# A decoder step on one Trainium2 core: reworked head, front, norms and router end, with eight products into an unread bank

## The reference

```
u = rmsnorm(h, norm_mix);  proj = u @ w_in          # rq rk rv rg | dqkv | dz | da db | gate_a gate_b
q, k = rotary(rq), rotary(rk);  o_r, s_ret = retention(q, k, rv)      # 4 heads, chunked
branch_a = (rms_plain(o_r) * silu(rg)) @ w_ret_up
conv = silu(causal_conv4(dqkv));  q, k = l2norm(..); g = -exp(a_log) softplus(da + dt_bias); beta = sigmoid(db)
o_d, s_dn = gated_delta(q, k, v, g, beta)           # triangular solve per chunk
branch_b = (rms_plain(o_d) * dn_norm * silu(dz)) @ w_dn_up
h += (sigmoid(gate_a) * branch_a + sigmoid(gate_b) * branch_b) @ w_out
u = rmsnorm(h, norm_ffn);  group = argmax(u @ w_router_group);  top 2 of the group's 4 experts
h += sum over chosen experts of weight * SwiGLU(u)  # 16 experts, 1024 -> 2x256 -> 1024
h += sigmoid(rmsnorm(h) @ w_ple_gate) * (p @ w_ple_proj);  y = rmsnorm(h, norm_final)
```

## Time and profile before

| | us |
|---|---|
| median of 3 runs | 942.37 (939.53 to 943.95) |
| profiled execution | 947.63, span 945.9 |
| TensorE busy | 902.4 |
| VectorE, ScalarE, GpSimd busy | 323.1, 226.9, 133.2 |
| mean granted TensorE clock | 0.977 of 2.4 GHz |
| DMA | 132.96 MB, 141 GB/s mean |

### The profile page before, as it was taken

How to read it: one execution, slowest core, us unless ns; L and a number is a source line. 1 busy time by engine, 2 the same in 40 slices (tenths; PEclk the granted TensorE clock), 3 DMA queues, 4 the chain that set the end, 5 groups by cost and what they waited for, 6 DMA issues and landing times.

```text
span 945.9 us, 11641 instructions
## 1 busy us (share of the span) xinstructions
PE 902.4 (95%) x4753; PEld 590.4 (62%) x4753; DVE 323.1 (34%) x709; ACT 226.9 (24%) x444; POOL 133.2 (14%) x161
## 2 busy tenths in 40 slices
PE   6999979999999999999999998997899999999996
PEld 3456747887889976777777774445444444444452
DVE  3213338876646322440100031334321111102553
ACT  3011325455222311330000001111021111114554
POOL 0423121040154315100000000001100000002100
PEclk9999979999999999999999999997899999999999
DMA  9204603202020202242022234001889999964211
GB/s 379 118 0 161 203 1 134 89 1 97 1 91 3 90 2 96 94 158 77 33 89 89 83 139 170 29 29 66 356 316 378 361 373 369 345 248 167 89 56 45
DMA packets 17764, 132.96 MB, mean 141 GB/s; under 512 B 2272, under 2 KB 2784, under 8 KB 10288
## 3 DMA queue, kind: packets, MB, share of 16 engines
q1 hardware_dynamic: 11600, 103.28, 28.5%
q0 software_dynamic: 5392, 26.38, 7.9%
q10 hardware_dynamic: 720, 2.56, 0.8%
HBM read 115.40 MB, written 21.01 MB: 144 GB/s over the span
## 4 chain that ended last, share of the span: by engine, by line
PE 91%; DVE 5%; ACT 2%; issue 1%; DMA 1%; POOL 0%; SPq 0%; ACTq 0%; DVEq 0%
PE pair L606 35%; PE single L1041 12%; PE pair L1132 7%; PE pair L658 7%; PE pair L952 7%; PE pair L1030 6%; PE pair L1074 2%; PE single L1020 1%; PE single L846 1%; PE single L824 1%; PE single L843 1%; PE single L801 1%; PE pair L752 1%; DMA mem<-in_xT 1%; DVE mem L1565 1%
## 5 line engine op out<-in xcount | busy, mean ns | idle before, releaser
L606 PE MATMUL pair<-mem 128*128 128x288 f32 x1408 | 351.4, 411 | 0.5 <-DVE mem L1675 0.5
L606 PEld LDWEIGHTS pair<-mem 128*128 128x128 f32 x1408 | 269.1, 192 | 80.1 <-issue 2.9
L1041 PE MATMUL single<-mem 128*128 128x512 f32 x256 | 115.3, 604 | 2.2 <-DVE mem L1843 2.2
L1041 PEld LDWEIGHTS single<-mem 128*128 128x128 f32 x256 | 48.3, 194 | 58.0 <-issue 55.2
L1153 ACT ACTIVATE mem<-single 128x256 f32<-128x256 f32 (+4 forms) x96 | 39.1, 416 | 133.4 <-PE single L961 57.4
L1153 ACT ACTIVATE mem<-pair 128x512 f32<-128x512 f32 (+5 forms) x79 | 35.1, 501 | 142.3 <-PE pair L606 64.7
L1132 PE MATMUL pair<-mem 128*128 128x512 f32 (+1 forms) x192 | 65.0, 534 | 1.4 <-DVE mem L1886 1.4
L952 PE MATMUL pair<-mem 128*128 128x512 f32 (+1 forms) x192 | 64.6, 527 | 1.7 <-DVE mem L1689 1.7
L658 PE MATMUL pair<-mem 128*128 128x512 f32 (+1 forms) x192 | 63.9, 524 | 0.4
L1030 PE MATMUL pair<-mem 128*128 128x512 f32 x128 | 57.7, 593 | 1.2 <-ACT mem L1153 1.2
L1836 DVE SCALAR_TENSOR_TENSOR mem<-single,mem 128x256 f32<-128x256 f32 x16 | 7.7, 484 | 146.9 <-PE single L1041 126.3
(11 more groups left out here) (341 smaller groups left out, 941.6 us busy)
## 6 DMA issues: line engine op xcount, KB each, us to landing
mem<-in_w_gu SPq DMA_DIRECT2D x16, 2048.0 KB, 9.2
mem<-in_w_down SPq DMA_DIRECT2D x16, 1024.0 KB, 11.6
y_slots<-mem SPq DMA_DIRECT2D x16, 512.0 KB, 3.1
y_slots<-in_zeros POOLq DMA_DIRECT2D x8, 512.0 KB, 8.3
mem<-in_w_ga SPq DMA_DIRECT2D x2, 2048.0 KB, 8.3
mem<-in_w_gb SPq DMA_DIRECT2D x2, 2048.0 KB, 9.0
mem<-in_w_wo SPq DMA_DIRECT2D x2, 2048.0 KB, 8.2
mem<-in_w_pg SPq DMA_DIRECT2D x2, 2048.0 KB, 11.7
```

Source lines behind the costliest of these rows:

```text
L606: last = nc.tensor.matmul(pb[:, hf, 0:HALF], w(k), rhs[:, k, hf * HALF:(hf + 1) * HALF], start=(k == 0), stop=(k == kk - 1))
L1041: last = nc.tensor.matmul(single[3][:, :], xT[u % 2][:, k, :], w_gu[u][:, k, :], start=(k == 0), stop=(k == KD - 1))
```

## The change

Head: x and the q|k weights come in pieces (HEADK), and the q|k products run block by block over all tiles (`tk`, blocks 0 to 5, then the sums of squares, block 6, `xr`, and block 7 tile by tile as `tmq`), in banks of their own; `qk` has five buffers. The front's steps are reordered. The expanded values are a step of their own (`vx`). gC takes all four prompt tiles in one product. The exponentials are a step for each tile, in blocks 9 and 10, and VectorE's part is `gX`. At level 32 VectorE subtracts in place and ScalarE copies. The addition in `oN` moves from TensorE to VectorE. `x2b` is evacuated by ScalarE, with the square behind it. At the router end eight products of ones by h2, 128x512, are written to a bank that nothing reads (`warm`); two tiles of `idv` go ahead of `x2b`, the others behind gate/up of expert 0; expert 1's transposes go into the middle of that gate/up.

```diff
 def schedule():
-    s = [("ss",)]
+    s = [("tk", k) for k in range(6)] + [("ss",), ("tk", 6), ("xr",)] + [("tmq", t) for t in range(NT)]
     for t in range(NT):
-        s += [("tmq", t)]
-        s += [("rTq", t - 1), ("rTk", t - 1)] if t else [("xr",)]
+        s += [("tmv", t)]
         if t >= 2: s += [("rO", t - 2), ("rU", t - 2)]
-        s += [("tmv", t)]
+        if t < 4: s += [("rTq", t), ("rTk", t)]
         if t: s += [("rS", t - 1)]
-    s += [("rTq", 4), ("rTk", 4), ("rO", 3), ("rU", 3), ("rS", 4)]
+    s += [("rTq", 4), ("rTk", 4), ("rO", 3), ("rU", 3), ("rS", 4), ("vx", 0), ("vx", 1)]
...
-               8: [("gG", t) for t in range(2, NT)] + [("gD", t) for t in range(2, NT)] + [("gE",)],
-               9: [("gs", t) for t in range(3)], 10: [("gs", 3), ("gs", 4)], 11: [("gr",)]}
+               8: [("gG", t) for t in range(2, NT)] + [("gD", t) for t in range(2, NT)],
+               9: [("gs", t) for t in range(3)] + [("gE", 0), ("gE", 1)],
+               10: [("gs", 3), ("gs", 4)] + [("gE", t) for t in range(2, NT)] + [("gX",)], 11: [("gr",)]}
...
-    s += [("x2b", z), ("rank", y), ("rt", z), ("ids", y), ("rtT", z)] + [("idv", t) for t in ORDER[:2]]
-    s += [("rank", z), ("ids", z), ("ovp", 1)] + [("idv", t) for t in ORDER[2:]] + [("cnt",)]
+    s += [("idv", t) for t in ORDER[:2]] + [("x2b", z), ("rank", y), ("rt", z), ("rtT", z), ("ids", y)]
+    s += [("warm", 0)] + [("rank", z)] + [("warm", 1)] + [("ids", z), ("cnt",)] + [("warm", i) for i in range(2, 8)] + [("ovp", 1)]
...
-            sp.dma_start(const[:, 0:HEAD], a["const"][:, 0:HEAD]).then_inc(sem("ld_head"), 16)
-            for k in range(0, KD, 2):
-                sp.dma_start(uT[:, k:k + 2, :], a["xT"][:, k:k + 2, :]).then_inc(sem(f"ld_x{k // 2}"), 16)
-            for k in range(0, KD, 4):
-                sp.dma_start(ring[0][:, 512 * k:512 * k + 2048], a["w_qk"][:, 512 * k:512 * k + 2048]).then_inc(sem(f"ld_qk{k // 4}"), 16)
+            for i, (lo, hi) in enumerate(HEADK):
+                sp.dma_start(uT[:, lo:hi, :], a["xT"][:, lo:hi, :]).then_inc(sem(f"ld_x{i}"), 16)
+                sp.dma_start(ring[0][:, 512 * lo:512 * hi], a["w_qk"][:, 512 * lo:512 * hi]).then_inc(sem(f"ld_qk{i}"), 16)
+                if i == 2:
+                    sp.dma_start(const[:, 0:HEAD], a["const"][:, 0:HEAD]).then_inc(sem("ld_head"), 16)
...
+                elif k0 in ("tk", "tmq"):
+                    k, tiles_ = (s[1], range(NT)) if k0 == "tk" else (KD - 1, [s[1]])
+                    pe.wait_ge(sem("xg"), k + 1)
+                    pe.wait_ge(sem(f"ld_qk{[k < hi for _, hi in HEADK].index(True)}"), 16)
+                    for t in tiles_:
+                        for rows, cols in sides(t):
+                            last = nc.tensor.matmul(q_bank[t][rows, cols], uT[:, k, t * P:t * P + ntok(t)],
+                                                    ring[0][:, 512 * k + cols.start:512 * k + cols.stop],
+                                                    start=(k == 0), stop=(k == KD - 1))
...
-                        if k0 == "oN":
-                            last = nc.tensor.matmul(pb[:, hf, 0:HALF], C("epsq").broadcast_to([P, P]), cs[:, s[1], h],
-                                                    start=False, stop=True)
+                elif k0 == "nq" and s[1] == "oN":
+                    dve.wait_ge(sem("nsq"), q + 1)
+                    dve.wait_ge(sem("q2"), m + 1)
+                    V.scalar_tensor_tensor(out=sq[q % 2], in0=cs[:, m, :], scalar=EPS * DK * DV, in1=sq[q % 2],
+                                           op0=ALU.mult, op1=ALU.add).then_inc(sem("osq"), 1)
...
-                    for t in range(NT):
-                        n = ntok(t)
-                        out = single[plan.buf[s]][0:n, 8 * t:8 * t + 8]
-                        nc.tensor.matmul(out[:, 0:4], tri(t), gl[0:n, t, :], start=True, stop=True)
-                        last = nc.tensor.matmul(out[:, 4:8], C("ones") if t < 4 else C("blk_s", 64), gl[0:n, t, :],
-                                                start=True, stop=True)
+                    for at, w_ in ((0, C("tri")), (16, C("ones"))):
+                        nc.tensor.matmul(out[:, at:at + 16], w_, gl[:, 0:4, :], start=True, stop=True)
+                    for at, w_ in ((32, C("tri_s", 64)), (36, C("blk_s", 64))):
+                        last = nc.tensor.matmul(out[0:64, at:at + 4], w_, gl[0:64, 4, :], start=True, stop=True)
...
+                elif k0 == "warm":
+                    nc.tensor.matmul(single[plan.buf[s]][:, :], C("ones"), h2[:, 0, 0:512], start=True, stop=True).then_inc(s_mm, 1)
...
+            def late_overflow_ids():
+                for t in ORDER[2:]:
+                    last = overflow_ids(t)
+                last.then_inc(sem("idv_mm"), 1)
...
                 for k in range(KD):
                     last = nc.tensor.matmul(single[3][:, :], xT[u % 2][:, k, :], w_gu[u][:, k, :], ...)
+                    if first and u == 0 and k == 3:
+                        xpose(xg_next[0], e + 1, u + 1)
                 last.then_inc(sem("gu_mm"), 1)
-                if nxt:
+                if nxt and not (first and u == 0):
                     xpose(xg_next[0], e + 1, u + 1)
-                if not (first and u == 0):
+                if first and u == 0:
+                    late_overflow_ids()
+                else:
                     down(e - 1, (u - 1) % 4, first and u <= 2)
...
+                elif k0 == "x2b":                     # ScalarE; was a VectorE copy
+                    copy(u2T[POS[t] % 2][:, 4:8, 0:n], ...).then_inc(ev(k0), 1)
                     nc.scalar.activation(sqj[0:n, :], h2[0:n, t, :], ACT.Square, accum_out=ms[0:n, 0, t:t + 1]).then_inc(sem("ms"), 1)
...
+                elif k0 == "lT" and s[1] == 32:       # ScalarE
+                    for r in blocks(t):
+                        last = copy(XT[t][r, :, r], XD[t][r])
+                    last.then_inc(sem("diag"), 1)
...
+                elif k0 == "vx":                      # GpSimd; was in rUs
+                    ev_wait(pool, ("tmv", 4))
+                    for c in range(2):
+                        G.tensor_tensor(vexp[h][0:64, c], ...).then_inc(sem("vexp"), 1)
```

More of the change, by code:

```diff
@@ L220, in __init__ @@
         self.order, self.mm, self.buf, self.before, self.chunk_last, self.norm = {}, {}, {}, {}, {}, {}
-        count, nmm, npair, nsingle, last = {}, 0, 0, 0, {}
+        count, nmm, npair, nsingle, last = {}, 0, 0, 1, {}
         for s in self.steps:
@@ L232, in __init__ @@
                 self.before[s] = None
+            if k in OWN:
+                last.update({key: s for key in own_banks(s)})
             if k in PAIR or k in SINGLE:
@@ L317, in build @@
         cnew = view(MISC + 288, NCONV, 27)
-        qk = [view(slot(0) + 512 * i, 512) for i in range(2)]
+        qk = [view(slot(i), 512) for i in (0, 1, 24, 25, 26)]
         rot = [view(slot(2) + 512 * i, 512) for i in range(2)]
@@ L457, in build @@
         idp = [pair[0][:, 1, 0:2 * NEXP], pair[1][:, 1, 0:8 * NEXP]]
+        q_bank = [pair[t // 2][:, t % 2, :] for t in range(4)] + [single[0]]
+        ss_bank = [single[1][:, 0:HALF], single[2][:, 0:HALF]]
+        xr_bank = single[3]
         def split(ap):
@@ L591, in bank_free @@
                 prev = plan.before[s]
-                if prev is not None:
+                if prev is not None and prev[0] != "warm":
                     ev_wait(pe, prev)
@@ L608, in gemm_channels, with overflow_ids @@
                 last.then_inc(s_mm, 1)
-            pe.wait_ge(sem("ld_head"), 16)
+            def overflow_ids(t):
+                i, n = POS[t], ntok(t)
+                pe.wait_ge(sem("pickm"), 1 if i < 2 else 2)
+                for j in range(2):
+                    at = 128 * (2 * i + j)
+                    last = nc.tensor.matmul(idp[1], pickm[0:n, i, j, :], eov[0:n, at:at + 128],
+                                            start=(i + j == 0), stop=(i + j == NT))
+                return last
             for s in STEPS:
@@ L1027, in down @@
                     pe.wait_ge(sem("y_ready"), 2 * e - 2)
+                elif u == 1:
+                    pe.wait_ge(sem("ids"), 4)
                 for n in range(2):
@@ L1162, in _ @@
                     mm_wait(act, s)
-                    nc.scalar.activation(split(rr[0]), pair576(s), ACT.Sqrt, bias=C("eps"), scale=1.0 / D).then_inc(ev(k0), 1)
+                    for hf in range(2):
+                        last = nc.scalar.activation(rr[0][:, hf * HALF:(hf + 1) * HALF], ss_bank[hf], ACT.Sqrt, bias=C("eps"), scale=1.0 / D)
+                    last.then_inc(ev(k0), 1)
                 elif k0 == "x2a":
@@ L1623, in _ @@
                         last = V.tensor_tensor(X[t][r], X[t][r], src[r], ALU.subtract)
-                    elif v < 32:
+                    else:
                         last = V.tensor_tensor(XD[t], XD[t], src, ALU.subtract)
-                    else:
-                        for r in blocks(t):
```

(1 more changed line is left out.)

155 lines of the change are left out of this document (77 added, 78 removed).

## The result

| | before | after |
|---|---|---|
| median | 943.16 (939.53 to 944.24, 4 runs) | 927.5 (926.08 to 929.0, 4 runs) |
| profiled execution | 947.63, span 945.9 | 926.82, span 925.1 |
| mean granted clock in it | 0.977 | 0.994 |

The ratio is 0.9841, interval 0.9808 to 0.9873: 15.7 us faster, where 27 were forecast. Faster was right; the time lies 4.5 us above the range.

The account below looks back on a forecast made before the run. TensorE's work (902.4 of 945.9 us busy), plus its idling and half clock, was taken as the bound. Eight terms summed to 27.2 us, taking the profiled 947.63 to 920.4; less 5.3 for the median gave 915, range 907 to 923.

Parts of the forecast that it names:

- terms 2: Expanded values moved ahead on GpSimd: TensorE's wait and the half clock behind it go, -10.1 us.
- 3: Cumulated gates (gC) in 4 products: fewer records and less half clock, -2.4 us.
- 4: Exponentials spread over two blocks: the key norms' wait and low clock go, against a new stall, -2.6 us.
- 6: Second norm (oN): each of four norms loses four of eight records, VectorE gets an extra step, -3.2 us.
- 7: Router, tiles 1 to 4: copy of the second half moves from VectorE to ScalarE, -0.5 us.
- term 8: Router end: overflow products moved, earlier gather, faster gate/up; -5 us, from -5.8 at full clock or -3.1 otherwise.
- rival B: Before the kk products: spread exponentials become a new wait, +3 instead of -2.6, 921 us; chance 0.15.
- C: Head starts at full clock and the clock stays full everywhere, 910 us; chance 0.12.
- rival A: Router end: clock falls despite the unread products, which delay the ids; gain 3.1 or less, 917 to 919; chance 0.2.
- Term 5: Inverse level 32: one VectorE subtract instead of two, ScalarE copies the blocks, -0.4 us.
- Sum of part 1: -3.0: Head and front: earlier block-by-block projection 5.1, shorter front waits 0.5, less 2.6 for half clock; bounds -6 and 0.
- The second step: Scaling the whole kernel's time: the profiled execution is 5.3 above the runs' median, so 920.4 becomes 915 us.

Follow-up runs that it names:

- e3: The changed kernel with the head and front of the kernel before; 925.65 us.
- e4: The changed kernel with its new head, but the front's steps in the order of the kernel before; 926.84 us.
- e7: The changed kernel with two more unread 512-column products in waits of the front; 923.61 us, in two groups.
- e6: The changed kernel without its eight products into the unread bank; 929.2 us.
- e13: The kernel before with the new head and front and nothing else of the change; 947.29 us, ratio 1.0049.
- e1: The changed kernel once more, unedited; 925.93 us.
- e9: The changed kernel with the two unread products of e7 in the front and the one of e5 at the router's end; 922.51 us.
- e10: e9 with three products of zeros ahead of the first query and key product; 920.84 us.
- e11: e9 with the middle four of the eight blocks of the query and key product made one; 921.23 us.
- e14: e9 with e11's blocks, products of zeros at the start and one unread product in the tail; 919.46 us, ratio 0.9756.
- e2: The kernel before once more, unedited; 944.82 us.
- e12: e5 with four products of zeros ahead of the row sums; 921.27 us.
- e5: e3 with one more unread product in the router's wait between the last router product and its transpose; 921.22 us.

## Why the prediction was wrong

**What held.** The sign, and terms 2, 3, 4, 6, 7 and 8 to within 1 us each in the profile (table above). Terms 2, 3, 4, 6 and 8 come to 24.3 against 23.3 forecast. The new wait of 1.2 before the kk products is there with 1.4 (L824), and rival B did not come. Nor did C: the first block ran at half clock. The router's end took the full-clock case, 6.0 against 5.8, in the profile; e3, e4 and e7 show that it can as well go the way of rival A, so that this term came in whole is partly luck. Term 5 cannot be read: between 260 and 287 us the profiles of the changed kernel and of e6, which are the same there, differ by 1.8.

**The step that failed: "Sum of part 1: -3.0".** It measured +4.4 in the profile, outside its bounds of -6 and 0, and +4.5 in the medians when alone (e13). No rival put a price on the clock in the front. The miss of 7.4 by its parts, from the rows of both profiles:

- "For the short waits there ... I take 0.5" gained. The waits in the front grew from 0.6 to 2.2, which misses by 2.1. In the new order a block's value product fills a bank, ScalarE empties it only after the state product of two blocks earlier has read the old values (the ScalarE row at 89.12, released by L763), and the scores want that bank. The old order is no cure: in e4, with the wide projections gone from between, the waits were 2.8 at another product.
- The clock in the front, which the sum did not price: 3.0. The records from 91.69 to 96.67 take 4.98 where before they took 3.06, and cv 0 takes 9.15 instead of 8.03. I priced the clock where TensorE starts, and never asked what the wide projections had been doing between the thin products of the front. The profiles of the changed kernel, e1, e6 and e13 have this half clock; in e7, e9, e10, e11 and e14, with wide products in the waits, cv 0 takes 8.03. In e4 it does too, without them, so the waits and thin products make the fall possible and not certain.
- "The projection's records are the same ones reordered": they are, but each follows one into another bank. The projection is 31.4 us of work before and 33.6 after, without the half clock of the first block: 2.2 (e11, for four of the eight blocks: 1.0).
- The first product came at 5.76, not 5.3: 0.5.
- The half clock of the first block, forecast at 2.6, cost 2.2 (5.91 instead of 3.70): 0.4 less.

These come to 2.1 + 3.0 + 2.2 + 0.5 - 0.4 = 7.4.

The Trainium skill, "TensorE: Matmul & The Clock Gate", section "Part 1: The HAM clock gate", says that how many of a kernel's first products are slow varies from run to run. The trace agrees: the same eight records took 5.09 (e4) to 6.75 us (e7) in the eight profiles of the new head without products of zeros.

**The second step: "It is 5.3 above the median ..., which gives 915."** The profile of before was slow because it held more half clock than is usual. Against e2, 2.2 us of that lay at the router's end, and term 8 removes them already, so they were taken off twice. Another 1.7 lay near 871, in no term, and is not there in the profile after either. So the changed kernel had no such excess to lose: its profile, 926.82, is just below its median of 927.5. The forecast's own sum for the profile was 920.4; with the head as measured it is 927.8.

**What stays open.** Why the clock falls in one execution and not in the next at the same rows was not tried; e3, e4 and e7 show only that it can fall at rows of the router's end that kept it in the changed kernel, where they come later (by 5.4 us against e3).

## What to carry to other kernels

A gain in one place moves every thin stretch behind it, and it can fall into half clock there; so a part's worth is read from its own stage in the trace, and the total only once the clock is pinned at all thin places (one wide unread product in each wait; here 1 us of products was worth 4.4). When a profiled execution is slower than the median, first ask which of its stretches made it so, and whether the change removes them, before any scaling. Wide products between thin ones can be cover for the clock as well as for latency: with the old head the front kept its clock in all six profiles, with the new head and order and nothing in the waits it lost it in all four.

## What the runs showed of the hardware

- The granted clock's rows show 1.00 in the first us of every run, while the first records take about twice as long (up to 1222 ns in the changed kernel, 592 for the same form from 12.18 on; 5.91 and 3.70 us for eight). Durations are the better witness.
- Products that change the bank and the tokens at every step cost some 70 ns more each than ones that stay (e11).
- Kernels whose clock was kept at the front and the router's end have narrow bands over 4 to 6 executions: e9 1.2, e12 1.3, e14 1.7, e5 2.1, e11 2.5, e10 2.9 us. Before has 10.6, though over 43 executions, and 4.7 over its first four.
